# A transformer block on one Trainium2 core: early modulation weights, value transfers, the merge's first inputs and the first expert's turning, all rearranged

## What is computed

```python
mod_x = silu(c) @ w_mod + b_mod            # (6144,): shifts, scales, gates
mod_c = silu(c_ctx) @ w_mod + b_mod
hx = modulate(rmsnorm(x, norm1_g), sh1, sc1)
zx = hx @ w_in + b_in                      # q, k, v, hyena inputs, two gates
kvc = hc @ w_in[:, COL_K:COL_G_HY] + ...   # keys and values of the context
hy = hyena_mixer(zx[:, :COL_Q], ...)       # two long convolutions, each gated
na = na_latent(q, k, v, kc, vc, rpb)       # 8 heads, 8 x 16 window on a 16 x 64 grid
mix = (sigmoid(g_hy) * (hy @ w_branch_hy) + sigmoid(g_na) * (na @ w_branch_na)) @ w_out
x = x + g1 * mix
aff = softmax(h2 @ w_router)               # each of 16 experts picks its 128 best tokens
g, idx = top_k(aff.T, 128);  x_e = h2[idx]
y_e = (silu(x_e @ w_gate) * (x_e @ w_up)) @ w_down     # D_FF = 2816
out = rmsnorm(x + g2 * scatter_add(idx, g * y_e), final_g)
```

## Time and profile before

| | |
|---|---|
| median of 3 runs | 2703.47 us (2702.67 to 2703.78) |
| profiled execution | 2703.3 us, span 2700.7 us |
| mean granted clock of PE | 0.973 of full |
| PE busy | 2545.6 us, 94% |
| DVE busy | 2121.3 us, 79% |
| ACT busy | 1469.9 us, 54% |
| POOL busy | 149.3 us, 6% |

### The profile page before, as it was taken

How to read it: one execution, slowest core, us unless ns; L and a number is a source line. 1 busy time by engine, 2 the same in 40 slices (tenths; PEclk the granted TensorE clock), 3 DMA queues, 4 the chain that set the end, 5 groups by cost and what they waited for, 6 DMA issues and landing times.

```text
span 2700.7 us, 32209 instructions
## 1 busy us (share of the span) xinstructions
PE 2545.6 (94%) x12577; PEld 2121.3 (79%) x12577; DVE 2121.3 (79%) x1976; ACT 1469.9 (54%) x1249; POOL 149.3 (6%) x159
## 2 busy tenths in 40 slices
PE   6999979999999899389999999999999999999997
PEld 2777869878878778368888888888888888888885
DVE  5674247667879555688888888889888888888887
ACT  4522136531121222177777777777777777777774
POOL 0011000011111000000000000000000000000000
PEclk9999989999999999689999999999999999999998
DMA  7498774464566733399999999999999999999994
GB/s 272 161 314 306 248 228 111 135 200 140 162 200 197 236 104 131 155 339 362 386 390 373 374 392 381 363 383 394 370 373 392 380 366 383 389 375 367 392 382 171
DMA packets 198628, 794.93 MB, mean 294 GB/s; under 512 B 17935, under 2 KB 65399, under 8 KB 128528
## 3 DMA queue, kind: packets, MB, share of 16 engines
q1 hardware_dynamic: 168196, 704.75, 69.4%
q0 software_dynamic: 30128, 88.11, 10.6%
q10 hardware_dynamic: 158, 0.07, 0.0%
HBM read 723.38 MB, written 69.48 MB: 294 GB/s over the span
## 4 chain that ended last, share of the span: by engine, by line
PE 53%; ACT 2%; issue 2%; DVE 1%; DVEq 0%; ACTq 0%
PE moe_ps_gate L2210 18%; PE moe_ps_up L2210 16%; PE moe_ps_y L2200 16%; PE moe_ps_h L2181 2%; ACT moe_w_hi L2251 1%; PE moe_ps_x L2173 1%; DVE raw L2373 0%; ACT moe_xt_hi L2244 0%; DVE moe_w_lo L2303 0%; DVE moe_h L2324 0%; ACT moe_sl L2264 0%; DVE raw L2360 0%; PE moe_ps_gate L2234 0%; PE moe_ps_gate L2236 0%; PE moe_ps_up L2234 0%
## 5 line engine op out<-in xcount | busy, mean ns | idle before, releaser
L2303 DVE TENSOR_TENSOR moe_w_lo<-raw,moe_w_hi 128x2048 fp32r<-128x2048 f32 x528 | 1207.6, 2290 | 159.8 <-ACT moe_w_hi L2251 159.6
L2251 ACT ACTIVATE moe_w_hi<-raw 128x2048 fp32r<-128x2048 f32 x528 | 1011.0, 1919 | 379.2 <-PE moe_ps_gate L2210 128.4
L2210 PE MATMUL moe_ps_up<-moe_w_hi,moe_xt_hi 128*128 128x512 f32 (+1 forms) x768 | 292.4, 381 | 0.0
L2210 PE MATMUL moe_ps_gate<-moe_w_hi,moe_xt_hi 128*128 128x512 f32 (+1 forms) x768 | 289.1, 376 | 1.4 <-DVE moe_xt_lo L2294 1.4
L2210 PE MATMUL moe_ps_gate<-moe_w_hi,moe_xt_lo 128*128 128x512 f32 (+1 forms) x768 | 286.5, 373 | 0.0
L2210 PE MATMUL moe_ps_up<-moe_w_hi,moe_xt_lo 128*128 128x512 f32 (+1 forms) x768 | 286.4, 373 | 0.0
L2210 PE MATMUL moe_ps_gate<-moe_w_lo,moe_xt_hi 128*128 128x512 f32 (+1 forms) x768 | 286.1, 373 | 0.0
L2210 PE MATMUL moe_ps_up<-moe_w_lo,moe_xt_hi 128*128 128x512 f32 (+1 forms) x768 | 285.9, 372 | 0.0
L2200 PE MATMUL moe_ps_y<-moe_w_hi,moe_ht_hi 128*128 128x512 f32 x704 | 218.5, 392 | 0.0
L2200 PE MATMUL moe_ps_y<-moe_w_hi,moe_ht_lo 128*128 128x512 f32 x704 | 217.0, 389 | 0.0
L2200 PE MATMUL moe_ps_y<-moe_w_lo,moe_ht_hi 128*128 128x512 f32 x704 | 217.0, 389 | 0.0
(11 more groups left out here) (278 smaller groups left out, 3707.1 us busy)
## 6 DMA issues: line engine op xcount, KB each, us to landing
raw<-in_w_moe SPq DMA_DIRECT2D x528, 1024.0 KB, 7.2
hyena_g_parts<-gw_d POOLq DMA_DIRECT2D x64, 512.0 KB, 4.7
proj_w_mod<-in_w_mod SPq DMA_DIRECT2D x32, 512.0 KB, 7.3
gw_d<-proj_g_parts POOLq DMA_DIRECT2D x16, 1024.0 KB, 7.4
w_in<-in_w_in SPq DMA_DIRECT2D x12, 1024.0 KB, 7.6
attn_table<-in_na_table SPq DMA_DIRECT2D x16, 576.0 KB, 5.6
norm_w_mod<-in_w_mod SPq DMA_DIRECT2D x16, 512.0 KB, 7.1
proj_g_raw<-in_w_in SPq DMA_DIRECT2D x16, 512.0 KB, 9.5
```

Source lines behind the costliest of these rows:

```text
L2210: mm = pe.matmul(ps, hp[:, e % 2, k, :], wp[:, r, :], start=(k == 0 and x == 0), stop=(k == KD - 1 and x == 2))
L2251: act.activation(w_hi[:, g % PARTS], raw[:, g % RAW], ACT.Copy).then_inc(hi_ready, 1)
L2303: dve.tensor_tensor(w_lo[:, g % PARTS], raw[:, g % RAW], w_hi[:, g % PARTS].bitcast(F32), ALU.subtract).then_inc(lo_ready, 1)
```

## The change

Four places are changed, together.

1. **Early modulation weights.** `w_early` gets places for all 16 pieces (under `h_hi` and `h_lo`, which aren't written yet), so `load_piece` waits for nothing. PE waits for a whole chunk before its first matmul, in chunks 0 to 2; the last chunk is waited for by pieces, on four semaphores that later transfers use too (`AFTER_PIECE` shifts their counts).
2. **Values.** `load_values` makes one transfer of 256 KB for each column block: its source is an access pattern of 4 grid rows by 32 tokens by 512 values, its destination 128 partitions. 16 transfers instead of 64.
3. **Merge.** Its tiles and semaphores are made before attention (`merge_places`). Hyena's last pass loads the first branch weights and three parts of na on SP's queue, with the fourth at its end; ScalarE copies the weights and the first na part ahead of that pass's outputs and the other three at the end of the block; DVE subtracts for the weights and the first na part between its last transform and the outputs. In the merge, DVE starts with na parts 1 to 3, ScalarE with y, and PE takes the attention branch first.
4. **First expert.** PE first does 36 transposes of the identity into `ps_x` (`WARM`). The second half of expert 0's tokens is turned into `ps_h`, with no wait between the halves. DVE takes each half's low part after its second subtraction, ahead of the third; PE starts unit 0 when the first half is there and unit 1 when the second is.

The diff, cut to its core:

```diff
-def load_values(sp, a, keep, kg):
+def load_values(eng, a, keep, kg):
     for b in range(4):
-        for r in range(4):
-            first = (4 * kg + r) * GRID_W + BAND_AT[b]
-            sp.dma_start(keep["v_band"][BAND * r:BAND * (r + 1), v_block(kg, b), 0:HEADS * HD],
-                         a["v_d"][first:first + BAND]).then_inc(keep["v_in"][kg // 3], 16)
+        first = 4 * kg * GRID_W + BAND_AT[b]
+        rows = bass.AP(a["v_d"].tensor, first * HEADS * HD, [[GRID_W * HEADS * HD, 4], [HEADS * HD, BAND], [1, HEADS * HD]])
+        eng.dma_start(keep["v_band"][:, v_block(kg, b), 0:HEADS * HD], rows).then_inc(keep["v_in"][kg // 3], 16)
...
-            f.sb("room", [P, 2112])
-            w_early = f.sb("w_mod", [P, PIECES, 2, 512])
...
+        last_piece_in = [g_in[0], g_in[1], b_mod_in, bv_in]
+        AFTER_PIECE = 16
+        CHUNK_IN = 16 * PIECES
...
                 def load_piece(n, q):
-                    if n:
-                        sp.wait_ge(piece_used, PIECES * (n - 1) + q + 1)
-                    sp.dma_start(w_early[:, q], mod_src[n, q]).then_inc(w_mod_in[q], 16)
+                    sp.dma_start(w_early[:, n, q], mod_src[n, q]
+                                 ).then_inc(last_piece_in[q] if n == NC - 1 else w_mod_in[n], 16)
...
+                    if n < NC - 1:
+                        pe.wait_ge(w_mod_in[n], CHUNK_IN)
                     for q in range(PIECES):
-                        pe.wait_ge(w_mod_in[q], 16 * n + 16)
+                        if n == NC - 1:
+                            pe.wait_ge(last_piece_in[q], 16)
                         for r in range(2):
                             k = 2 * q + r
-                            mm = pe.matmul(ps_early[STRIP * r:STRIP * r + 2, n % 2, :], c_silu[:, k, :], w_early[:, q, r, :],
+                            mm = pe.matmul(ps_early[STRIP * r:STRIP * r + 2, n % 2, :], c_silu[:, k, :], w_early[:, n, q, r, :],
                                            start=(q == 0), stop=(q == PIECES - 1))
...
-                        pe.wait_ge(v_in[g], 16 * 48 if g == 0 else 16 * 16)
+                        pe.wait_ge(v_in[g], 16 * 12 if g == 0 else 16 * 4)
...
+                def load_na(k):
+                    s = k % NA_SLOTS
+                    if k >= NA_SLOTS:
+                        sp.wait_ge(na_lo_ready, k - NA_SLOTS + 1)
+                    sp.dma_start(coming["na_raw"][:, s], a["na_d"][k]).then_inc(na_in, 16)
...
+                        if p == PASSES - 1 and r == 1:
+                            sp.wait_ge(tap_used, PH * PASSES)
+                            sp.wait_ge(a_done, a_at["seg", p, PH - 1] + 1)
+                            for b, w in enumerate(branch_sources(a)):
+                                sp.dma_start(coming["b_raw"][:, 0, b], w[0]).then_inc(branch_in[0], 16)
+                            for k in range(NA_SLOTS):
+                                load_na(k)
...
+                load_na(NA_SLOTS)
...
+                def high_na(k):
+                    act.wait_ge(na_in, 16 * max(NA_SLOTS, k + 1))
+                    act.activation(coming["hi"][1][:, k], coming["na_raw"][:, k % NA_SLOTS], ACT.Copy
+                                   ).then_inc(na_hi_ready, 1)
...
+                    if p == PASSES - 1:
+                        act.wait_ge(branch_in[0], 32)
+                        act.activation(coming["b_hi"][:, 0], coming["b_raw"][:, 0], ACT.Copy).then_inc(bh_ready, 1)
+                        act.wait_ge(out_done, NB * p)
+                        high_na(0)
...
+                for k in range(1, 4):
+                    high_na(k)
...
+                    if p == PASSES - 1:
+                        dve.wait_ge(bh_ready, 1)
+                        dve.tensor_tensor(coming["b_lo"][:, 0], coming["b_raw"][:, 0], coming["b_hi"][:, 0].bitcast(F32),
+                                          ALU.subtract).then_inc(bl_ready, 1)
+                        low_na(dve, coming, 0)
...
+def low_na(dve, at, k):
+    dve.wait_ge(at["in_hi_ready"], k + 1)
+    dve.tensor_tensor(at["lo"][1][:, k], at["na_raw"][:, k % NA_SLOTS], at["hi"][1][:, k].bitcast(F32), ALU.subtract
+                      ).then_inc(at["in_lo_ready"], 1)
...
                 pe.wait_ge(bl_ready, 3)
-                branch(0, 0, 0, first=True)
-                branch(0, 1, 0)
+                branch(0, 0, 1, first=True)
+                branch(0, 1, 1)
                 for th in range(2):
-                    branch(0, th, 1, first=not th).then_inc(branched, 1)
+                    branch(0, th, 0, first=not th).then_inc(branched, 1)
...
-                for b, src in enumerate((y_t, na_t)):
-                    if b:
-                        split(0, 0, 0)
-                        act.wait_ge(na_in, 64)
-                    for k in range(4):
-                        act.activation(in_hi[:, b, k, :], src[:, k, :], ACT.Copy).then_inc(in_hi_ready, 1)
+                for k in range(4):
+                    act.activation(in_hi[0][:, k, :], y_t[:, k, :], ACT.Copy).then_inc(in_hi_ready, 1)
...
+                for k in range(1, 4):
+                    low_na(dve, at, k)
+                for k in range(4):
+                    dve.wait_ge(in_hi_ready, 4 + k + 1)
+                    dve.tensor_tensor(in_lo[0][:, k, :], y_t[:, k, :], in_hi[0][:, k, :].bitcast(F32),
+                                      ALU.subtract).then_inc(in_lo_ready, 1)
...
+        WARM = 36
...
+        def x_turned(e, half):
+
+            return ps_h if (e, half) == (0, 1) else ps_x
...
                 def turn_x(e, half):
-                    if half or e:
+                    if e:
                         pe.wait_ge(x_parts, 2 * e + half)
                     if half == 0:
                         pe.wait_ge(gathered, 16 * e + 16)
                     for k in range(4):
                         at = (4 * half + k) * P
-                        mm = pe.transpose(ps_x[:, k * P:(k + 1) * P], xe[:, at:at + P], ident[:])
+                        mm = pe.transpose(x_turned(e, half)[:, k * P:(k + 1) * P], xe[:, at:at + P], ident[:])
...
+                for n in range(WARM):
+                    pe.transpose(ps_x[:, n % 4 * P:(n % 4 + 1) * P], ident[:], ident[:])
                 turn_x(0, 0)
                 turn_x(0, 1)
                 for e in range(E_N):
-                    pe.wait_ge(x_parts, 2 * e + 2)
+                    if e:
+                        pe.wait_ge(x_parts, 2 * e + 2)
                     for u in range(N_U):
+                        if e == 0 and u < 2:
+                            pe.wait_ge(x_parts, u + 1)
...
-                for g in range(AHEAD):
+                split(0)
+                split(1)
+                for half in range(2):
+                    low_x(0, half)
+                for g in range(2, AHEAD):
                     split(g)
```

More of the change, by code:

```diff
@@ L228, in norm_and_project @@
         ps_mod = m.psum("ps_mod", [P, 512])
+        w_early = keep["w_early"]
         small_in, SMALL = sems("small_in"), 16 * 14
@@ L1203, in hyena @@
         decay_in, gate_in, v2_in = keep["w_mod_in"][0:3]
+        coming = keep["merge"]
+        branch_in, na_in, na_hi_ready, na_lo_ready, bh_ready, bl_ready = (
+            coming[n] for n in ("w_in", "na_in", "in_hi_ready", "in_lo_ready", "bh_ready", "bl_ready"))
         LOADED = 16 * MOD_CHUNKS
@@ L2417, in program @@
                 y_t = Maker(nc, mixer).sb("y_t", [P, 4, T])
+                keep["merge"] = merge_places(nc, sems)
                 n = Maker(nc, convolving)
```

79 lines of the change are left out of this document (43 added, 36 removed).

## The result

The changed kernel takes 2711.82 us (median; 2708.72 to 2713.21), the kernel before 2702.71 us on the same terms: a ratio of 1.0036, with a 95% interval of 1.0027 to 1.0045. That is 9 us slower, where I had forecast 7 us faster; it lies outside my range of 2675 to 2701 us. The profiled execution took 2711.0 us for a span of 2709.2 us.

What follows compares the result with a forecast made beforehand. TensorE, busy for 94% of the span, was taken as the bound, with time to win only at joints between stages. The terms -3.4 + 8 - 5.6 - 6.2 = -7.2 us took 2703.3 us to 2696 us, range 2675 to 2701 us.

Steps and rivals of the forecast that it cites:

- The four engines: Values' loads: each new transfer, outermost count 4, runs on 4 engines and takes 2.7 us; likeliest case, 2696 us, chance 0.77.
- the PEclk line: Earlier profile: PE's clock read as halved near the start, a sixth and a third of the way in, before the experts.
- Joint B: Values, from projection into attention: the new transfers cost 8 us, between 4 and 12.
- The last four values, the second table and head 2 follow in the queue: Attention: these later loads arrive by about 403 us and are wanted about then; no further cost counted.
- Attention's first scores could start at 361 us: End of the projection block: GpSimd's last store is the next limit, so attention starts at 361 us instead of 373.26.
- may be held back by the four full queues: Values' loads: SP's issues might be delayed by full queues; no size given.
- Joint D: Start of the first expert: a gain of 6.2 us, 3.8 from the earlier start and 2.4 from the clock.
- DVE's third and fourth splits come 3.5 and 1.7 us late against the old order but 2 us before PE wants them: First expert: VectorE's later weight splits slip by 3.5 and 1.7 us but still come 2 us before PE wants them.
- Joint A: Early modulation weights, at the kernel's start: a gain of 3.4 us, between 1.5 and 4.2.
- a joint's gain arrives almost whole: All four places between stages: what is gained or lost there reaches the kernel's end almost whole.
- Joint C: From hyena into the merge: a gain of 5.6 us, from 3 to 6.8, allowing at most 3 us for half clock.
- The rival that ended at 2713 us: Values' loads: four engines deliver less than 24 GB/s each; at 16 GB/s the kernel takes 2713 us; slower case, chance 0.08.

Runs made afterwards that it cites:

- the run with transposes: The kernel before with only the early modulation pieces changed, plus 24 identity transposes while TensorE waits for the last modulation row: 2698.65 us against 2700.60 us.
- in pairs: The kernel before with 32 value transfers of 128 KB, each of one grid row and two column blocks: 2699.62 us against 2701.92 us, ratio 0.9997.

## Why the prediction was wrong

**What held.** The four engines, read from one short row: the share of 0.26 at 98 GB/s is theirs, and the first product came at 384.79 us (forecast: 387.5). That row (a share of 0.06) was thin evidence for a count of 4, and the runs with counts of 32 and 2 are what bears it out. The Trainium skill's rule (DMA: Bandwidth & Descriptors, "Why a DMA increments its semaphore by 16 and not by 1"), by which the largest number up to 16 that divides the outermost counts of both sides sets how many engines work, is borne out by all three cases here: 0.26 for 4, 0.13 for 2, near 1 for 32. The gains at joints A and C had the right sign and place. One reading was wrong without weight in the sum: the PEclk line of the earlier trace rows is low only in its sixth slice, before the experts and at the very end; the falls "near the start" and "a third of the way in" are too short to show in it (the second is that of the earlier trace rows).

**Joint B, 8 us forecast, 16.9 measured.** Three steps failed, and the first did the damage.
- "The last four values, the second table and head 2 follow in the queue (to about 403 us by the same rates) and are wanted about then." They were wanted much sooner: the fifth product needs the last values, four steps of some 2.3 us behind the first. The products of both kernels side by side: the fourth is 4.1 us behind (393.29 against 389.23), the fifth 10.0 us (401.48 against 391.48, the 5.78 us wait), the sixth 12.0 us (half clock: 0.50 from 401.4 to 405 us), the eighth 15.4 us (ScalarE waits 2.40 us for head 2's keys, with probability copies queued behind it, and PE waits 2.96 us for those), the ninth 16.2 us. The kernel before had its fifth product 9.6 us behind its first. By that pace the fifth product wanted the last values at about 394.4 us; PE had them only at 401.48. I added up the first wait and took the later ones for covered without setting the time of need beside the time of arrival.
- "Attention's first scores could start at 361 us." GpSimd's last store ends the block only at 369 us, which the run with its stores on ScalarE shows. In the changed kernel this didn't decide, since SP was later still (374.15 us).
- SP's issues "may be held back by the four full queues" stood there as a remark with no price. They took 47.6 us. The block's end waits for SP, so this put attention's start 13 us behind what I took, though the first product, which waited for the data, hid it.

**Joint D, 6.2 us forecast, 0.6 measured.** Start and clock came as forecast (first gate matmul 8.5 us behind the block's start, at full clock). The failed step is "DVE's third and fourth splits come 3.5 and 1.7 us late against the old order but 2 us before PE wants them". I looked at the splits, and not at what stands behind ten of them on VectorE, the first multiplication. In the kernel before it ended at 1182.0 us and PE used it at 1182.10: there was no slack at all. So PE's gain of 6.5 us at this place, about what I had forecast, was cut to the 3.4 us by which VectorE itself came sooner, and the fall of the clock behind the stall took all but 0.6. With VectorE's steps in another order the same change gives 6.9 us.

**Joint A, 3.4 us forecast, 0.8 measured.** 2.5 us of it came (the columns at 42.35 us; I had 41.4, because chunk 1's row was added by DVE at 25.57 us, 1.1 us sooner than before, not 2.0). The failed step is the assumption that a joint's gain arrives almost whole: 1.8 us were lost behind the columns, where the clock was at half from 43.9 to 50.7 us in steps that ran at full in the profile before. I had put no term for the clock here. PE's wait before the columns had become 2.97 us. That the wait is the cause fits the run with transposes, but isn't shown: a low clock came up here in two profiles with the unchanged start as well.

**Joint C, 5.6 us forecast, 7.2 measured.** I had allowed for a fall of the clock. It didn't come, and the DMA time of the five loads cost nothing that can be seen in the trace.

**The sum.** -3.4 + 8 - 5.6 - 6.2 = -7.2 was forecast, -0.8 + 16.9 - 7.2 - 0.6 = +8.3 measured. The values' term was sized at half of what they cost. Two terms carry the miss, B by 8.9 us and D by 5.6 us. The rival that ended at 2713 us had the right time for a wrong reason: it wanted engines slower than 24 GB/s, and they moved 24.5. What would have deserved its chance is the mechanism above, a second and a third wait in the same queue.

## What to carry to other kernels

When a transfer becomes slower, list every later customer of the same queue with the time when it is wanted and the time when it arrives; the first wait is seldom the only one. Before a step is pulled forward, look at which engine's work reaches PE with no slack in the stretch behind it, and at what is queued ahead of that work: a head start beyond that slack, and beyond what that engine itself gains, turns into a wait until the order is changed too. Give every transfer an outermost count that 16 divides on both sides, and let GpSimd issue nothing late in a block that others wait to leave.

## What the runs showed of the hardware

- A transfer on SP's queue moved 24.5 GB/s for each engine where it ran on 2 or 4 of them (49 and 98 GB/s). On all 16 it was 24 GB/s an engine with the large transfers of 128 outer rows (383 GB/s at a share of 1.05), and 16 with the values' smaller ones (261 GB/s at 1.06 in pairs, beside GpSimd's stores; 142 GB/s at 0.54 in the kernel before). Why the small ones are slower is open.
- Where the transfers ran on four engines, one issue took SP about 2.7 us (13 of them 35.21 us) instead of 0.48.
- A block whose last store GpSimd issued at 359.5 us ended at 369 us, some 2.5 us behind the store's landing; with that store issued by ScalarE it ended at 361 us, 5 us ahead of the landing.
- The same wait of 3.0 to 3.1 us in the first expert was followed by PE's clock at half for 6.4 us in one profile (3.02 us), for some 3.4 us in another (3.06 us, the changed kernel with the small transfers) and not at all in a third (3.07 us).
- With 24 transposes of the identity, while PE had nothing to do, the clock was at full from 42 to 51 us in that profile; with 36 the first gate matmul ran at full clock. They cost nothing that the traces show.
